# A router behind the last mixer: tokens transposed and logits taken inside the output projection, rows normalised token-major, the pick table made by GpSimd

## The reference, cut to what matters

```python
x = x + y                                   # y: the mixer's output projection
h = rms_norm(x, norm_ffn[1])
probs = softmax(h @ w_router + b_router)
top_p, top_i = lax.top_k(probs, 2)
top_p = top_p / sum(top_p)
gates = sum(one_hot(top_i, 8) * top_p)
for e in range(8):
    y = y + gates[..., e] * swiglu(h, w_gu[e], w_down[e])
x = x + y
```

## Time and profile before

| | us |
|---|---|
| runs: median of three (lowest, highest) | 1679.86 (1679.72, 1682.17) |
| the profiled execution | 1678.39 |
| its span | 1676.3 |

### The profile page before, as it was taken

The page is one execution under the profiler, slowest core; times in us unless marked ns, Lnnn a source line. Parts: engine busy times, 40 slices in busy tenths (PEclk is TensorE's granted clock), DMA queues, the critical chain, the costliest instruction groups (busy, mean ns, idle before and its releaser), DMA issues.

```text
span 1676.3 us, 22958 instructions
## 1 busy us (share of the span) xinstructions
PE 1628.0 (97%) x8599; PEld 1261.1 (75%) x8599; DVE 1197.3 (71%) x1200; ACT 980.3 (58%) x839; POOL 115.2 (7%) x159
## 2 busy tenths in 40 slices
PE   8999999999998999799999999999999999999996
PEld 6986799999897867577777777677677677677774
DVE  6534456654645443788888888888888888888886
ACT  5513343323422333577877877877777778778774
POOL 2011000000111130100000000000000000000010
PEclk9999999999997999799999999999999999999998
DMA  8445345445442153699999999999999999999992
GB/s 253 128 150 172 115 151 172 161 148 170 145 140 62 47 87 101 212 380 374 352 386 382 354 384 378 359 380 372 370 376 363 380 374 364 383 372 351 394 375 81
DMA packets 232438, 448.40 MB, mean 267 GB/s; under 512 B 15836, under 2 KB 82448, under 8 KB 232384
## 3 DMA queue, kind: packets, MB, share of 16 engines
q1 hardware_dynamic: 224224, 421.27, 70.5%
q0 software_dynamic: 7488, 24.01, 5.3%
q10 hardware_dynamic: 672, 2.36, 0.4%
HBM read 433.04 MB, written 14.57 MB: 267 GB/s over the span
## 4 chain that ended last, share of the span: by engine, by line
PE 94%; DVE 3%; ACT 1%; issue 1%; DMA 0%; POOL 0%; DVEq 0%; SPq 0%; ACTq 0%; POOLq 0%
PE bank L888 25%; PE bank L890 25%; PE bank L889 25%; PE bank L882 8%; PE bank L1402 1%; PE bank L873 1%; PE bank L977 1%; PE bank L1100 1%; PE bank L1030 1%; PE bank L1066 1%; PE bank L1053 1%; PE bank L1042 1%; ACT h_tok L1704 0%; PE bank L1211 0%; PE bank L1209 0%
## 5 line engine op out<-in xcount | busy, mean ns | idle before, releaser
L2392 DVE TENSOR_TENSOR w_lo<-ring,w_hi 128x2048 fp32r<-128x2048 f32 x336 | 767.8, 2289 | 126.1 <-ACT w_hi L1740 125.7
L1740 ACT ACTIVATE w_hi<-ring 128x2048 fp32r<-128x2048 f32 x336 | 643.3, 1918 | 225.7 <-PE bank L890 225.4
L888 PE MATMUL bank<-w_hi,xg_hi 128*96 128x512 f32 x896 | 356.5, 398 | 3.8 <-DVE w_lo L2392 3.8
L890 PE MATMUL bank<-w_hi,xg_lo 128*96 128x512 f32 x896 | 354.6, 396 | 0.0
L889 PE MATMUL bank<-w_lo,xg_hi 128*96 128x512 f32 x896 | 352.5, 393 | 0.0
L888 PE MATMUL bank<-work_split 128*128 128x288 f32 (+2 forms) x840 | 247.4, 295 | 4.7 <-DVE work_split L2038 2.6
L888 PEld LDWEIGHTS bank<-w_hi,xg_hi 128*96 128x96 f32 x896 | 145.0, 162 | 64.1 <-DVE w_lo L2392 5.9
L890 PEld LDWEIGHTS bank<-w_hi,xg_lo 128*96 128x96 f32 x896 | 144.9, 162 | 63.1
L889 PE MATMUL bank<-work_split 128*128 128x288 f32 x648 | 191.2, 295 | 0.0
L890 PE MATMUL bank<-work_split,ring_lo 128*128 128x288 f32 x648 | 190.8, 294 | 0.0
L889 PEld LDWEIGHTS bank<-w_lo,xg_hi 128*96 128x96 f32 x896 | 145.4, 162 | 60.2
(11 more groups left out here) (420 smaller groups left out, 1848.0 us busy)
## 6 DMA issues: line engine op xcount, KB each, us to landing
ring<-in_moe_w_gu_dram SPq DMA_DIRECT2D x224, 1024.0 KB, 7.2
ring<-in_moe_w_down_dram SPq DMA_DIRECT2D x112, 1024.0 KB, 7.0
ring<-in_ffn_w_gu_dram SPq DMA_DIRECT2D x22, 1024.0 KB, 5.0
ring<-in_gla_w_in_dram SPq DMA_DIRECT2D x12, 1024.0 KB, 10.6
ring<-in_mlstm_w_in_dram SPq DMA_DIRECT2D x12, 1024.0 KB, 5.2
ring<-in_ffn_w_down_dram SPq DMA_DIRECT2D x8, 1024.0 KB, 5.1
out_dram<-work POOLq DMA_DIRECT2D x9, 512.0 KB, 3.4
ring<-in_gla_w_out_dram SPq DMA_DIRECT2D x4, 1024.0 KB, 5.1
```

The lines of the kernel that those rows point to most:

```text
L888: pe.matmul(out, w_hi_, x_hi, start=first, stop=False, skip_group_check=True)
L890: return pe.matmul(out, w_lo_, x_hi, start=False, stop=last, skip_group_check=True)
L1740: ac.activation(w_hi[:, j % SPLIT, :], src, ACT.Copy).then_inc(whi_ready, 1)
L2392: ve.tensor_tensor(w_lo[:, j % SPLIT, :], src, w_hi[:, j % SPLIT, :].bitcast(F32), ALU.subtract)\
```

## The change

- The gain of the norm is multiplied into the router's weights once (in layer 0), so that logits can be taken from `xT` itself. `hm`, the sum of squares over partitions, and the transposes of `hm` are gone.
- Behind the tiles 2 to 7 of the projection PE transposes the blocks of `xT` that are complete (`token_tile`) and takes their share of the logits, summed in bank 2 over all of the projection. The transposed blocks use banks 0 and 1 in turn.
- ACT copies each transposed block to `x_acc`, squares the rows of `x_acc` in two parts (768 and 256 columns) with a sum along the row, and takes the inverse root for three columns of 128 tokens. DVE multiplies `x_acc` by the gain, loaded as a row to all partitions (`g_ffn`), into `h_tok`, and ACT scales `h_tok` in place, three instructions of 1024 columns.
- Top-2 is taken from the logits; the two gates come from the exponential of their difference. The three searches have no wait between them.
- The ranks are four products in place of twelve. Positions are kept with BIG added, which saves two steps.
- The number of items is ready by itself (`items_ready`); the item table is made by POOL after it has issued the stores of `x_rows` and `h_rows`, as seven values side by side with a product and halving sums. DVE and SP wait for it (`table_ready`) where they use it.
- The first piece of a pass is loaded, and split, at the end of the pass before; the first piece of the first pass is split in the router, beside the gather. One further piece is loaded and split at the end of the last pass.
- The first tokens' high part is made by DVE in place of ACT.

The diff, cut to its core:

```diff
@@ SP
+            load_first(0, 1)
             with sp.Fori(1, NE - 1) as e:
-                load_pass(e, e)                      # for j in range(PER)
+                load_pass(e, e)                      # for j in range(1, PER)
+                load_first(e, e + 1)
             sp.wait_ge(table_ready, 1)
+            sp.wait_ge(items_ready, 1)
...
@@ GpSimd
+            gp.dma_start(g_ffn, ins["norm_ffn"][1:2, :].broadcast_to([P, D])).then_inc(g_loaded, 16)
...
             for kt in range(KT):
-                gp.wait_ge(*copied(f"Mh{kt}"))
-            token_rows(h_rows, h_tok, rows_stored)
-            for kt in range(KT):
                 gp.wait_ge(*copied(f"Mx{kt}"))
             token_rows(x_rows, x_acc, rows_stored)
+            gp.wait_ge(h_scaled, TT)
+            token_rows(h_rows, h_tok, rows_stored)
...
+            gp.wait_ge(gates_ready, 1)
+            gp.wait_ge(pick_ready, 1)
+            gp.tensor_copy(tab_f[:, 0:NE], expert_no[:, :])
+            gp.memset(tab_f[:, NE + MORE:15], 0.0)
+            gp.tensor_copy(cand_v[:, 0, :, :], cand_e[:, :, :])
+            gp.tensor_tensor(cand_v[:, 1:1 + TT, :, :], ..., ALU.subtract)
+            table_step(gp.tensor_copy(cand_v[:, 1 + TT:, :, :], ...))
+            table_step(gp.tensor_tensor(picked[:, :, :, :], pick..., cand_v..., ALU.mult))
+            for n in (8, 4, 2):
+                table_step(gp.tensor_tensor(picked[:, :, :, 0:n], picked[:, :, :, 0:n], picked[:, :, :, n:2 * n], ALU.add))
+            last_sum(pos3[:, :, NE:NE + MORE], slice(1, 1 + TT))
+            last_sum(gate3[:, :, NE:NE + MORE], slice(1 + TT, n_values))
+            table_step(last_sum(tab_f[:, NE:NE + MORE], 0))
+            gp.tensor_copy(tab_i[:, 0:15], tab_f[:, 0:15]).then_inc(table_ready, 1)
             gp.wait_ge(rows_zero, 16)
             gp.wait_ge(rows_stored, 96)
-            gp.wait_ge(table_ready, 1)
@@ TensorE
+        token_after = {2: (0,), 3: (1, 2), 4: (3,), 5: (4,), 6: (5,), 7: (6, 7)}
+            def token_tile(kt):
+                pe.wait_ge(*copied(f"L1w{kt}"))
+                bk = begin(f"Mx{kt}")
+                for tt, (t0, n) in enumerate(TS):
+                    mm = pe.transpose(bk[0:n, tt * P:(tt + 1) * P], xT[:, kt, t0:t0 + n], ident[:, :])
+                end(mm, f"Mx{kt}")
...
+                for tt, (t0, n) in enumerate(TS):
+                    mm = pe.matmul(bk[0:n, tt * NE:(tt + 1) * NE], xT[:, kt, t0:t0 + n], w_rt[:, kt, :], ...)
-            out_proj("L1", num, 8)
-            norm(3, "Mss")
...
+            for m in out_tiles("L1", out_proj("L1", num, 8)):
+                for kt in token_after[m]:
+                    token_tile(kt)
             pe.wait_ge(chosen_ready, 1)
             bk = begin("Mrank")
+            pe.matmul(bk[:, 0:TT * NE], before[:, :], chosen[:, :, :], start=True, ...)
             for s in range(TT):
+                mm = pe.matmul(bk[:, (s + 1) * NE:(TT + 1) * NE]..., ones[:, :], chosen[:, s, :]..., start=False, ...)
...
-            pe.wait_ge(table_ready, 1)
+            pe.wait_ge(gates_ready, 1)
             end(item_rows(begin("Mgt")), "Mgt")
+            pe.wait_ge(items_ready, 1)
@@ ScalarE
-            norm(3, "Mss", "L1w", "L1r7", None, late=0)
+            ac.wait_ge(tok_cleared, 2)
+            for kt in range(KT):
+                bk = take(f"Mx{kt}")
+                ac.activation(x_acc[:, 0:2, cols], bk[:, 0:2 * P]..., ACT.Copy)
+                free(ac.activation(x_acc[0:NSM, 2, cols], bk[0:NSM, 2 * P:3 * P], ACT.Copy), f"Mx{kt}")
+                if kt in (KT - 3, KT - 1):
...
+                        ac.activation(squares[0:n, tt, cols], x_acc[0:n, tt, cols], ACT.Square, bias=zero[0:n],
+                                      accum_out=st[0:n, part, tt:tt + 1]).then_inc(rsq_ready, 1)
+            ac.wait_ge(rmean_ready, 1)
+            ac.activation(r_tok[:, :], st[:, 2, :], ACT.Abs_reciprocal_sqrt, bias=zero).then_inc(rinv_ready, 1)
+            ac.wait_ge(r_ready, 1)
+            ac.wait_ge(hg_ready, KT)
+            for tt, (t0, n) in enumerate(TS):
+                ac.activation(h_tok[0:n, tt, :], h_tok[0:n, tt, :], ACT.Copy, scale=r_tok[0:n, tt:tt + 1]).then_inc(h_scaled, 1)
             ac.wait_ge(logit_ready, 1)
+            ac.activation(st[:, 0, :], st[:, 5, :], ACT.Exp, bias=zero).then_inc(prob_ready, 1)
+            ac.wait_ge(*full("L1w7"))
+            weight_hi(0, 0, first=True)
...
-                for j in range(PER):
+                for j in range(1, PER):
+                    weight_hi(j, i)
...
+                weight_hi(0, i + 1)
@@ VectorE
+            residual("L1w", (0, 1))
...
+            for m in range(2, KT):
+                residual("L1w", (m,))
+                for kt in token_after[m]:
+                    token_gain(kt)
+            ve.wait_ge(rsq_ready, 2 * TT)
...
+            select(lambda tt: slice(tt, tt + 1), sel_ready)
...
+            ve.tensor_copy(tab_i[:, 15:16], tab_f[:, 15:16]).then_inc(items_ready, 1)
+            ve.wait_ge(prob_ready, 1)
...
+            ve.tensor_copy(gate_token[:, :, 0:1], gates[:, :, 0:1]).then_inc(gates_ready, 1)
+            step(ve.tensor_tensor(o16, o16, f16, ALU.mult))
+            ve.tensor_tensor(pick[:, :, :], ..., ALU.is_equal).then_inc(pick_ready, 1)
+            weight_lo(0, 0)
             for half in range(2):
                 bk = take(f"Mga{half}")
+                ve.tensor_copy(xg_hi[:, 4 * half:4 * half + 4, :], bk...).then_inc(hi_ready, 1)
                 ve.wait_ge(hi_ready, half + 1)
                 free(tokens_lo(half, bk), f"Mga{half}")
-            copy_residual((2, 4, 5, 6, 7))
...
                     if due == ("g", 1, 0):
+                        ve.wait_ge(table_ready, 1)
...
+                weight_lo(0, i + 1)
```

More of the change, by code:

```diff
@@ L980, in out_proj, with out_tiles @@
                             end(mm, f"{l}w{m}")
+                return src
+            def out_tiles(l, src):
                 for m in range(2, 8, 2):
-                    tiles([f"{l}w{m}", f"{l}w{m + 1}"], src)
+                    w = weights().rearrange("p (k n) -> p k n", k=KT)
+                    for a in range(2):
+                        name = f"{l}w{m + a}"
+                        bk = begin(name)
+                        end(rows_of(bk, w, src, a * P, KT, P), name)
+                        yield m + a
+            def token_tile(kt):
[4 more added lines that the diff above has]
+                end(mm, f"Mx{kt}")
+                if kt == 0:
+                    begin("Mlog")
+                    pe.wait_ge(w_rt_scaled, 1)
+                bk = psum[uses["Mlog"][0]]
+                for tt, (t0, n) in enumerate(TS):
+                    mm = pe.matmul(bk[0:n, tt * NE:(tt + 1) * NE], xT[:, kt, t0:t0 + n], w_rt[:, kt, :],
+                                   start=(kt == 0 and tt == 0), stop=(kt == KT - 1), skip_group_check=True)
+                    if kt == 0 and tt < 2:
+                        mm.then_inc(split_used, 1)
+                if kt == KT - 1:
+                    end(mm, "Mlog")
             first_tile()
@@ L1124, in _ @@
             r_tile("L0", 7)
-            out_proj("L0", o0, 0)
+            for m in out_tiles("L0", out_proj("L0", o0, 0)):
+                pass
             for c in range(FBLK):
@@ L1345, in first_bank @@
                 return uses[f"Mga{half}"][0]
-            for kt in range(KT):
-                pe.wait_ge(*copied(f"Mh{kt}"))
+            pe.wait_ge(h_scaled, TT)
             pe.wait_ge(sel_ready, 1)
@@ L1693, in _ @@
                 gate("L1", m, ACT.Sigmoid)
-            norm(3, "Mss", "L1w", "L1r7", None, late=0)
-            ac.wait_ge(logit_ready, 1)
-            ac.activation(pr[:, :, :], lg[:, :, :], ACT.Exp, bias=zero).then_inc(prob_ready, 1)
-            ac.wait_ge(tok_cleared, 1)
-            ac.wait_ge(*copied("Mrt"))
-            for kt in range(KT):
-                bk = take(f"Mh{kt}")
-                for tt, (t0, n) in enumerate(TS):
-                    ins_ = ac.activation(h_tok[0:n, tt, kt * P:(kt + 1) * P], bk[0:n, tt * P:(tt + 1) * P], ACT.Copy,
-                                         scale=r_tok[0:n, tt:tt + 1])
-                    if tt == TT - 1:
-                        free(ins_, f"Mh{kt}")
-                    else:
-                        step(ins_)
@@ L2323, in picked_value @@
-            def picked_value(out, v16):
-                step(ve.tensor_tensor(picked[:, :, :], pick[:, :, :], v16.unsqueeze(1).broadcast_to([P, MORE, 2 * NE]), ALU.mult))
-                step(ve.tensor_reduce(out, picked[:, :, :], AX_X, ALU.add))
-            step(ve.tensor_copy(tab_f[:, 0:NE], expert_no[:, :]))
-            step(ve.memset(tab_f[:, NE + MORE:15], 0.0))
-            picked_value(tab_f[:, NE:NE + MORE], e16)
-            for tt in range(TT):
-                step(ve.tensor_tensor(cand_v[:, :, :], place[:, tt, :].unsqueeze(1).broadcast_to([P, 2, NE]), cand_skip[:, :, :], ALU.subtract))
```

(3 more changed lines are left out.)

191 lines of the change are left out of this document (103 added, 88 removed).

## The result

| | us |
|---|---|
| changed kernel: median of four runs (lowest, highest) | 1659.58 (1656.82, 1660.21) |
| kernel before beside it: median of four | 1681.01 (1679.72, 1684.48) |
| ratio, 95% interval | 0.9874 [0.9853, 0.9895] |
| profiled execution of the changed kernel, its span | 1660.21, 1657.9 |

Of the page's slices of TensorE, the one from 670 to 712 us goes from 7 to 9 tenths and the one before it from 9 to 8; the others are as before.

The account below looks back on a forecast made before the run. TensorE was taken to bound the kernel, so an earlier expert loop carries to the end: 1678.4 - 15.7 + 0.1 = 1662.8 us, with 1.5 us for the median 1664.3, stated as 1664.0; range 1661 to 1668.5.

Parts of the forecast that it names:

- last tile ends: Output projection with six of eight token blocks between its tiles: last tile ends at 658.0 us, bounds 657.4 to 660.4.
- chosen experts: Router's top-2 without waits between searches: 2.0 us after the logits, at 666.3 us; bounds 1.7 and 2.6.
- gather starts: Router, after the ranks: the gather starts at 669.1 us instead of 675.71.
- low part 0 ends: VectorE beside the gather: low part of the first weight piece takes 2.2 us and ends at 673.9 us.
- third piece: Start of the expert loop on TensorE: third weight piece at 684.3 us instead of 699.99.
- the item number: Before the first expert product: reading it costs VectorE 1.1 us, and TensorE the same.
- GpSimd's table: Item table moved from VectorE to GpSimd: 3 to 6.5 us, done by 680, at no cost.
- Rival 1: Clock is down at the expert loop's start: 2.0 us more, less 0.4 of waiting, 1666 us; chance 0.13.
- rival 3: Router's ScalarE chain is longer than its rows, gather starts 3 to 5 us later: 1667 to 1669 us; chance 0.10.
- rival 4: Light products between projection tiles drag the clock down: up to 23.4 us more, 1687; chance 0.03 in a slower form.
- the ranks: Router, after top-2: four products, eight records of 0.22 us, 1.5 us with the start, ending at 667.9.
- the sum: Whole kernel: profiled 1678.4 us less 15.7 gained up to the third piece, plus 0.1, gives 1662.8.

Follow-up runs that it names:

- e4: Changed kernel with all eight transposed blocks and their logits behind the projection instead of between its tiles; 1663.35 us, ratio 0.9906.
- e7: Changed kernel with GpSimd's 560-column product of the item table made seven times instead of once; 1664.64 us, ratio 0.9912.
- e12_before_small: Kernel before with only its two scratch buffers moved into the working area's free end, so that area begins 384 bytes lower; 1676.70 us, ratio 0.9977.
- e8_best: Changed kernel plus an early dummy inverse root, in a newly declared buffer, and 11 and two unused products in TensorE's waits before ranks and gather; 1662.76 us, ratio 0.9893.
- e6_warm: Changed kernel plus 12 unused TensorE products of 288 columns between the last logits and the ranks; 1659.27 us, ratio 0.9875.
- e14_best2: Changed kernel plus 11 and two unused TensorE products before ranks and gather, and a dummy inverse root written into an existing buffer; 1657.13 us, ratio 0.9850.

## Why the prediction was too careful by 4 us

Each step, counted from the start of the last six tiles (628.59 before, 626.43 after):

| step | predicted | measured |
|---|---|---|
| last tile ends | 29.4 | 29.6 |
| logits ready | 35.7 | 35.8 |
| chosen experts | 37.7 | 37.7 |
| gather starts | 40.5 | 40.7 |
| gather takes | 7.47 | 7.60 (8.8 in four of eight profiles) |
| low part 0 ends | 45.3 | 45.2 |
| first expert product | 49.7 | 49.7 |
| third piece | 55.7 | 55.4 |
| third piece earlier by | 15.7 | 16.0 here, 15.3 as a mean |

The mechanism and its terms held. One that was off: the item number costs VectorE 0.39 us and not the 1.1 us taken from the earlier trace rows (that row puts the idle time down to ScalarE's high part, but the three high parts ran from 686.10 to 691.61, so the first had long been done; what made it 1.1 there stays open), and TensorE nothing, since it waits for the tokens' second half, ready at 49.5 (49.1 predicted). GpSimd's table took 6.85 us including 2.10 behind the low part (3 to 6.5 were expected, ended by 680; it ended at 676.38), and nothing waits for it. That it ends ahead of low part 1 is luck: predicted was up to 0.8 us of it left beside that part. Rival 1 didn't come: the clock is up at the loop's start. Nor did rival 3 (the chain has its twin at the end of the kernel, to 0.1 us) or rival 4: no tile is slow; but e4 shows its premise right, since the same blocks in a row were followed by the lower level. Two small sums were off and cancelled: eight records of 0.22 us are 1.8 us and not the 1.5 put down for the ranks (1.88 measured), and from there to the gather it was 1.06 us, not 1.2.

The Trainium skill, "GPSIMD Engine Reference", section 3.1, gave an estimate of 1.3 us for the 560-column product; the trace agrees, 1.39. "SBUF — State Buffer", section "SBUF: two separate sides", has the port pair of VectorE and GpSimd as an exclusive lock; e7 agrees from both sides, 3.33 us for that product beside low parts and 15.55 us for five low parts beside GpSimd.

**The step that failed** is the sum: "1678.4 - 15.7 + 0.1 = 1662.8". It carries everything ahead of the router over from the kernel before at no change, and the range had no term for it either. The diff removes two declarations ahead of the working area, and I costed only instructions. Moving that area by 384 bytes brings a product down from 132.2 to 131.1 ns; for 1968 products that is 2.2 us. The dense layer's 1584 of them took 212.96 us in the first profile before and 211.29 in the changed one, and the arrivals of this pair differ by 2.16 us. With it the sum is 1662.8 - 2.2 = 1660.6, against a profiled 1660.21; the router's 16.0 in place of 15.7 is the rest.

The median was missed by 4.4 us, more than that. Another 1.8 us come from the step behind the sum: I set the median 1.2 us above it, because the profiled execution before ran below the median of three, and the changed kernel's ran 0.6 us above its own. That is scatter between executions, which no profile of one of them could tell. So: 15.3 us are the router's, and 2.2 (the pitch alone) to 3.8 (the median of e12_before_small, with what the clock adds) the place's. The sum of 17.5 to 19.1 us lies among the 17 to 21 us that the three ratios of the changed kernel give; they tell no finer.

A second fault is the range. It was built on three runs of the kernel before that covered 2.5 us; with 12 and 10 runs it covers 8. What stays open is why the place changes the pitch, and whether a place is better than the changed kernel's: four others were tried, no more.

## What to carry to other kernels

A diff that adds or removes a buffer moves all that is declared behind it. Count a matmul stretch that waits for nothing, in both kernels, before a gain or a loss is put down to the edited part; here 1% of pitch hid behind a TensorE busy for 100% of the time, and the place (1.7% of pitch, and the clock's falls that came with it) turned a good edit (e8_best) into no gain. Where TensorE idles for a microsecond ahead of heavy work, the price can include the clock afterwards, and cheap products into an unread bank took it away here once they covered both gaps and not the longer one alone.

## What the runs showed of the hardware

- A product of 288 columns from `work_split`, at a clock of 1.00 and without waits, comes every 131.1, 132.2 or 133.3 ns by where the working area lies (0; +64, +128 or +384; +32 bytes), the same in every profile of a place (ten, six and four).
- An idle gap of 1.06 us ahead of the gather was followed by the lower level some 1.5 us into it (e6_warm); 1.22 us of products in the same gap kept the upper one (e14_best2). The idle 0.98 us before the first expert product, behind a gather that ended at the upper level, was followed by no fall.
- One and the same gather takes 5.57, 7.6 or 8.8 us, with a clock of 1.00 throughout, at the lower level for the first 4.35 us, or for longer (0.50 and 0.73 in its two halves).
- GpSimd's product over 560 columns takes 1.38 us alone and 3.33 us beside VectorE's low parts, and these take 3.1 us each beside it in place of 2.29 (e7_pool6).
